# Decode attention on one Trainium2 core: the differential value products spread over four column strips and summed by one more product

## What is computed

```
s = q . k / 8 - slope * distance       # 2 kv heads x 2 query heads x 2 maps
p = softmax(s)                         # over the 1025 keys
a = p[map 0] - lam * p[map 1]
o = a @ v                              # v: 2 kv heads x 128 columns per token
o = rmsnorm(o) * subln * (1 - lam_init)
```

## Time and profile before

| | us |
|---|---|
| median of 3 runs | 2084.87 |
| lowest and highest run | 2082.83, 2086.28 |
| span of the profiled execution | 2086.2 |
| TensorE busy in that span | 1972.7 |
| VectorE busy | 1163.0 |
| ScalarE busy | 678.2 |
| POOL busy | 152.2 |

### The profile page before, as it was taken

The page is one execution under the profiler, slowest core; times in us unless marked ns, Lnnn a source line. Parts: engine busy times, 40 slices in busy tenths (PEclk is TensorE's granted clock), DMA queues, the critical chain, the costliest instruction groups (busy, mean ns, idle before and its releaser), DMA issues. The chain is left out here.

```text
span 2086.2 us, 34791 instructions
## 1 busy us (share of the span) xinstructions
PE 1972.7 (95%) x13032; PEld 1856.5 (89%) x13032; DVE 1163.0 (56%) x2531; ACT 678.2 (33%) x1273; POOL 152.2 (7%) x190
## 2 busy tenths in 40 slices
PE   5889999999997799999998999999999999999997
PEld 4658798789996688898898999999999999999997
DVE  4944333334244677777775546655556565555555
ACT  5623243331223566666573133311111110101011
POOL 1442100101300100000200000000000000000000
PEclk8799999999998899999899999999999999999999
DMA  9776453521001000000003541221212020211102
GB/s 311 255 215 205 152 180 98 156 94 60 30 26 66 1 1 1 1 1 1 1 1 102 173 131 50 62 61 30 60 30 60 30 60 30 60 31 59 40 0 82
DMA packets 151758, 157.10 MB, mean 75 GB/s; under 512 B 15859, under 2 KB 132483, under 8 KB 151604
## 3 DMA queue, kind: packets, MB, share of 16 engines
q1 hardware_dynamic: 140076, 130.73, 20.4%
q0 software_dynamic: 4656, 16.40, 2.3%
q10 hardware_dynamic: 6912, 8.46, 1.1%
HBM read 139.33 MB, written 18.32 MB: 76 GB/s over the span
## 5 line engine op out<-in xcount | busy, mean ns | idle before, releaser
L1877 DVE SCALAR_TENSOR_TENSOR l_x2T<-tail_bank,g_modT,l_x2T 128x344 f32<-128x344 f32 (+1 forms) x528 | 265.3, 566 | 101.5 <-PE tail_bank L1614 101.3
L1614 PE MATMUL tail_bank<-l_wo 128*128 128x344 f32 x1584 | 270.2, 319 | 1.8 <-DVE late_total_s L1883 1.8
L1614 PEld LDWEIGHTS tail_bank<-l_wo 128*128 128x128 f32 x1584 | 252.7, 188 | 2.0 <-issue 2.0
L1448 ACT ACTIVATE l_act<-tail_bank 128x344 f32<-128x344 f32 x66 | 30.2, 457 | 523.6 <-PE tail_bank L1596 523.6
L884 PE MATMUL nsa_out<-zs_z,nsa_probT 128*128 128x64 f32 (+1 forms) x1344 | 176.1, 277 | 5.3 <-DVE zs_z L1040 5.1
L884 PEld LDWEIGHTS nsa_out<-zs_z,nsa_probT 128*128 128x128 f32 x1344 | 169.1, 198 | 7.1 <-DVE zs_z L1040 7.0
L1596 PE MATMUL tail_bank<-late_words_hi,l_uhi 128*128 128x344 f32 x528 | 169.7, 321 | 3.3 <-DVE late_words_lo L1780 3.3
L1596 PE MATMUL tail_bank<-late_words_lo,l_uhi 128*128 128x344 f32 x528 | 169.3, 321 | 0.0
L1596 PE MATMUL tail_bank<-late_words_hi,l_ulo 128*128 128x344 f32 x528 | 169.2, 320 | 0.0
L1596 PE MATMUL tail_bank<-late_words_lo,late_wo 128*128 128x344 f32 x528 | 169.1, 320 | 0.0
L1596 PE MATMUL tail_bank<-late_words_hi,l_wo 128*128 128x344 f32 x528 | 169.1, 320 | 0.0
(11 more groups left out here) (504 smaller groups left out, 4329.2 us busy)
## 6 DMA issues: line engine op xcount, KB each, us to landing
mod_wr<-in_w_ada SPq DMA_DIRECT2D x24, 1024.0 KB, 5.3
kin_kin<-in_cache_kv SPq DMA_DIRECT2D x64, 256.0 KB, 3.4
late_gate<-in_w_ffn_in SPq DMA_DIRECT2D x22, 512.0 KB, 5.7
l_raw_o<-in_w_ffn_out SPq DMA_DIRECT2D x22, 512.0 KB, 3.6
late_raw<-in_w_ffn_in SPq DMA_DIRECT2D x22, 512.0 KB, 5.4
gate_d<-dec_gate ACTq DMA_DIRECT2D x48, 172.0 KB, 2.9
late_gate<-gate_d SPq DMA_DIRECT2D x8, 1032.0 KB, 5.5
dec_vin<-in_cache_kv SPq DMA_DIRECT2D x64, 128.0 KB, 2.2
```

Source lines behind the costliest of these rows:

```text
L1448: act.activation(sg[(j + c) % 2], pg[(j + c) % 2][:, 0:TCH], ACT.Silu).then_inc(silu_done, 1)
L1614: mm = pe.matmul(po[u % 4][:, 0:TCH], w[j][:, k * P:(k + 1) * P], a[j][:, tok(c)], start=(q == 0), stop=(q == 2))
L1877: mm = dve.scalar_tensor_tensor(out=here, in0=po[u % 4][:, 0:part_w(c)], scalar=g.modT[:, 5 * KD + k, NDEC:NC9], in1=here, op0=ALU.mult, o ...
```

## The change

The page products of one part go to four strips of 32 output partitions each, page `t` to strip `t % 4`, so that a strip adds up two pages; the new token's row is added to strip 0. The stationary operand is 32 columns wide in place of 16: the second half is the next page's scores, whose products lie in partitions that nothing uses. ScalarE copies the whole bank into a `kT` buffer that is free at that time (`odf_copied`), and one product with a constant matrix `fold` (128 x 16, ones where the partition belongs to that output row) adds the four strips into `odf[0:16]` (`folded_values`). The copy stands at the next pair's `h = 0` ahead of the squares, the sum product at its `h = 1` ahead of the transposes; for the last pair the copy stands behind ScalarE's last loop step and the sum product ahead of the second early unit. `outputs` waits for the sum product, and so does the `kT` copy that would overwrite the buffer. VectorE builds `fold` once.

```diff
+        fold = s.sb("fold", [P, R])
...
+        odf_sb, odf_sum, folded = s.sem("odf_sb"), s.sem("odf_sum"), s.sem("folded")
+        spread = [kT[((p + 1) * NY + 2) % 3] for p in range(NP)]
...
+                def odf_copied(p):
+                    act.wait_ge(pv, 2 * p + 2)
+                    act.wait_ge(kt_used, (p + 1) * NY)
+                    act.activation(spread[p][:], odf[:], ACT.Copy).then_inc(odf_sb, 1)
...
+                        if h == 0 and p:
+                            odf_copied(p - 1)
                         if 0 <= h < 4:
                             squares(p, h // 2, h % 2)
...
+                            if h == 3 and p:
+                                act.wait_ge(odf_sum, p)
                             act.activation(kT[at % 3][:], kt[at % 2][:], ACT.Copy).then_inc(kt_sb, 1)
...
+                odf_copied(NP - 1)
                 gates(HALVES // 2 - 1)
...
-                            pe.matmul(odf[0:R, :], sco[:, S_DIF + t * R:S_DIF + (t + 1) * R], vin[:, :, t, :], start=(t == 0), stop=False)
+                            rows = slice(t % 4 * 32, t % 4 * 32 + 32)
+                            pe.matmul(odf[rows, :], sco[:, S_DIF + t * R:S_DIF + (t + 2) * R], vin[:, :, t, :], start=(t < 4), stop=(t > 4))
                         if part == 3:
-                            pe.matmul(odf[0:R, :], new(S_DIF + NPAGE * R), vnew[:, 256:768], start=False, stop=True).then_inc(pv, 1)
+                            pe.matmul(odf[0:32, :], sco[0:1, S_DIF + NPAGE * R:S_DIF + (NPAGE + 2) * R], vnew[:, 256:768],
+                                      start=False, stop=True).then_inc(pv, 1)
+
+                def folded_values(p):
+                    pe.wait_ge(folded, 1)
+                    pe.wait_ge(odf_sb, p + 1)
+                    pe.matmul(odf[0:R, :], fold[:], spread[p][:], start=True, stop=True).then_inc(odf_sum, 1)
...
+                    if h == 1 and p:
+                        folded_values(p - 1)
                     if 1 <= h < 1 + NY:
                         transposed(p, h - 1)
...
                 for t in range(Z_AHEAD):
+                    if t == 1:
+                        folded_values(NP - 1)
...
                     dve.wait_ge(pv, 2 * p + 2)
+                    dve.wait_ge(odf_sum, p + 1)
...
                 norms()
+                dve.tensor_reduce(fold[:], g.ident[:].rearrange("p (j r) -> p r j", j=4)[:, 0:R, :], AX.X, ALU.add).then_inc(folded, 1)
```

## The result

| | before | after |
|---|---|---|
| median, us | 2086.74 | 2098.38 |
| lowest and highest | 2082.83, 2094.52 | 2095.19, 2101.61 |
| runs | 12 | 12 |
| span of the profiled execution | 2086.2 | 2096.7 |
| PE busy in that span | 1972.7 | 1969.6 |

The ratio is 1.0047, with a 95% interval from 1.0036 to 1.0059: some 9.8 us slower, where 12.4 were forecast. That the forecast came so near is partly luck, as the rows show.

The account below looks back on a forecast made before the run. The prediction took PE (TensorE) to bound the decode stage. Costs 2.9 + 0.3 + 6.6 + 3.0 + 7.9 + 2.0 = 22.7 less a gain of 10.3 gave +12.4 us on 2084.87, or 2097, range 2084 to 2108.

Parts of the forecast that it names:

- parts under 1.2 us: Sign of failure: the prediction fails if a part of four page products on PE takes under 1.2 us.
- The strips: Page products on PE in the decode stage: in-order overlap, five slots in place of eight, -10.3 us, bounds 0 and -20.6.
- full overlap: Rival, chance 0.25: all four strips' page products run together, gain 20.6 against costs of 22.7, +2.1 us or 2087.
- The low clock: Lower granted clock behind PE's stalls at pairs 1 and 3: 1.5 us each, +3.0; pair 2 pays already.
- The stalls: PE waits ahead of second scores because `outputs` starts 4.4 us later: 2.2 each at pairs 1, 2, 3, +6.6 us.
- The end of the stage: VectorE's chain after the last pair starts 12.2 us later and ends behind PE; the stage ends +7.9 us later.
- cold start: PE starts the next stage at low clock after 7 us of idleness: +2.0 us, at least 0.
- Sum products: One per pair on PE, 0.96 us each; three in the loop, +2.9 us, the fourth in the stage's end.
- ScalarE's copies: Four 128x512 copies from PSUM, one per pair: cost nothing; without cover 0.58 us each.
- The fold matrix: VectorE's added reduction at the stage's start, on the way to the first transposes: +0.3 us, between nothing and 1.47.
- No overlap: Rival, chance 0.22: page products in different strips do not overlap and nothing is saved, +22.7 us or 2107.
- half-price waits: Rival, chance 0.05: waits cost half of what was priced, 8 us less, about 2089.

Follow-up runs that it names:

- the repeats: Three more profiled runs: two of the unaltered changed kernel, 2097.34 and 2096.90 us, and one of the changed kernel with all pages in strip 0, 2112.23 us.
- the waits alone: Kernel before, products unchanged, with `outputs` made to wait about as late as in the changed kernel: 2114.43 us against 2085.96, ratio 1.0122.
- the second repeat: The unaltered changed kernel profiled a third time, for the length of the low clock: 2096.90 us.
- both moves with one strip: Changed kernel with loop sum products one half-step earlier, last pair's copy and sum product at half-step 92, all pages in strip 0: 2094.49 us, ratio 1.0031 to before.
- The move at the end alone: Changed kernel with only the last pair's copy and sum product moved up to half-step 92: 2086.36 us against 2087.35 for the kernel before, ratio 0.9999.
- both moves: Changed kernel with loop sum products one half-step earlier and the last pair's copy and sum product at half-step 92: 2070.34 us against 2087.35 before, ratio 0.9918.

## Why the prediction was right, and where it was not

The prediction named parts under 1.2 us as a sign of its failure, and they take 1.00: on the strips it was wrong. Its time came out all the same because a second term was wrong in the opposite direction, which is luck. The waits it had right.

- **The strips** were mis-sized: "If order of start is kept, only the second pass of one strip and the first of the next can run together" gave 5 slots of 8 and -10.3. The rows show 2 of 8 and -20.3; two strips show 4 of 8. That step assumed that a product's two passes stand next to one another and hold the later ones up. The rows show the four first passes together and the four second ones after; in which order they are queued no run shows. The prediction had full overlap as its bound of -20.6. The Trainium skill's page "TensorE: Matmul & The Clock Gate", section "Measured speedup vs the span model", says that products in different column strips take the span of one and about 4 ns more per tile. This trace agrees for products of two passes, with 7 ns between the starts in place of 4: one such product alone costs 0.97 here, and four in four strips 1.00.
- **The low clock** was mis-sized the other way: 3.0 forecast, 9.3 in the profile. It was priced from one stretch of before, of 1.5 lost, with 2.0 as the most that a stall would cost; pair 1 cost 6.3 and pair 3 cost 3.0. In the repeats it cost 0 to 7 per stall, by half the lengths in the table. Nor do 0.75 us lie at an edge: in three traces (the waits alone, the second repeat, both moves with one strip) pair 0's stall of 0.77 was followed by 3.4 us at 0.50, and in two others a stall of 1.94 by none. The two errors, -10.0 and +6.3, cancel in good part. That is why full overlap, which was the rival priced at 2087, still ended near the forecast's 2097.
- **The stalls** were right in place, cause and size: 2.0, 2.2 (beyond the 0.75 of before) and 2.0 measured, 6.2 in all for 6.6 (its own rows give 2.1 and not 2.2 for pair 1: 267.9 - 265.8). Holding `outputs` back alone makes them, and moving the sum product takes them away; with the waits in the rows above, the chain through VectorE's `outputs` to ScalarE's key copy is shown.
- **The end of the stage** was right: 7.8 for 7.9, with VectorE last in place of PE, and 1.7 for the 2.0 of the cold start (1.3 to 2.8 in the other kernels that stall there). The move at the end alone took PE's wait ahead of the next stage back to 0.72.
- **Sum products** cost 0.97 each for 0.96. **ScalarE's copies** take 0.60 each; with both moves pair 2's stall is 0.75 as before and no other appears, so they delay nothing on PE that shows there. The fold matrix costs some 0.1 in the profiles, for 0.3.
- **No overlap** is excluded by the first row of the trace, and **half-price waits** by the stalls' sizes.

## What to carry to other kernels

Splitting an accumulation over column strips was a real gain on this TensorE-bound stage (20.3 us), and the extra sum products were cheap (3.9); what decided is where that product stands, since its consumer's queue waits with it. Before pricing such a product by its length, follow what is queued behind its reader back to TensorE, and place it as early as its input allows: here one half-step in the loop and a few at the stage's end turned +9.8 us into -17. A stall on the bound engine can cost more than its length, here by 0 to 7 us and not the same in every run, so give it a range and not a value.

## What the runs showed that was not expected

- fp32 products of two passes in four column strips run fully together: 3.54, 1.84 and 1.00 us for four products in one, two and four strips.
- After a stall of about 2 us the granted clock stayed at 0.50 for 0 to 14 us in the same program, though PE was busy behind it.
- A stall of 0.75 to 0.77 at pair 2 was followed by a lower clock in the profile of before, and by a clock of 1.00 in those with the loop's sum product moved; at pair 0 the same stall was followed by either.
